# One level of a chunk's triangular block inverse moved from the second to the first stage of a software pipeline

## What is computed

```python
    gdiff = jnp.where(causal, g[..., :, None] - g[..., None, :], 0.0)
    decay = jnp.where(causal, jnp.exp(gdiff), 0.0)
    k_beta = k * beta[..., None]
    lower = jnp.where(strict, jnp.einsum('bhncd,bhnsd->bhncs', k_beta, k) * decay, 0.0)
    rhs = jnp.concatenate([v * beta[..., None], k_beta * jnp.exp(g)[..., None]], axis=-1)
    sol = lax.linalg.triangular_solve(lower, rhs, left_side=True, lower=True, unit_diagonal=True)
    u, w = sol[..., :dv], sol[..., dv:]
    intra = jnp.where(causal, jnp.einsum('bhncd,bhnsd->bhncs', q, k) * decay, 0.0)
    def step(state, inp):
        u_i, w_i, q_i, k_i, a_i, cd_i = inp
        v_new = u_i - jnp.einsum('bhcd,bhde->bhce', w_i, state)
        o_i = jnp.einsum('bhcd,bhde->bhce', q_i, state) + jnp.einsum('bhcs,bhse->bhce', a_i, v_new)
        state = state * cd_i[..., None, None] + jnp.einsum('bhcd,bhce->bhde', k_i, v_new)
        return state, o_i
```

## Time and profile before

| what | value |
|---|---|
| median of 3 runs | 1527.27 us (1525.84 to 1528.35) |
| span of the profiled execution, first to last instruction | 1523.0 us |
| TensorE busy | 1427.9 us, 94% |
| VectorE busy | 674.3 us, 44% |
| GpSimd busy | 624.9 us, 41% |
| ScalarE busy | 452.2 us, 30% |
| mean granted TensorE clock | 0.965 of full speed |

### The profile page before, as it was taken

One profiled execution on the slowest core, in us unless ns is written; L12 is line 12 of the kernel. 1 busy time (PEld: TensorE's weight loads), 2 busy tenths in 40 slices (PEclk: granted clock), 3 DMA queues, 4 the chain that ended last, 5 costly groups with the idle time before them and its releaser, 6 DMA issues.

```text
span 1523.0 us, 18439 instructions
## 1 busy us (share of the span) xinstructions
PE 1427.9 (94%) x7019; PEld 1191.1 (78%) x7019; DVE 674.3 (44%) x857; ACT 452.2 (30%) x516; POOL 624.9 (41%) x359
## 2 busy tenths in 40 slices
PE   3899999999979999889979999999999999999996
PEld 3477878878768999876858888888888888888884
DVE  3825152342656666435553343424243342343426
ACT  3326345351722222133323131221212122131223
POOL 4357667586724111114335252433425234252430
PEclk8799999999989999979989999999999999999998
DMA  8043424233110001101102111111201112111102
GB/s 334 16 125 95 106 56 130 69 89 90 55 56 1 1 0 55 56 28 40 58 0 71 41 56 41 41 41 51 73 28 55 41 41 69 41 55 41 41 28 111
DMA packets 122348, 92.36 MB, mean 61 GB/s; under 512 B 3903, under 2 KB 110668, under 8 KB 122316
## 3 DMA queue, kind: packets, MB, share of 16 engines
q1 hardware_dynamic: 122316, 91.94, 20.0%
HBM read 87.73 MB, written 4.19 MB: 60 GB/s over the span
## 4 chain that ended last, share of the span: by engine, by line
PE 81%; DVE 8%; ACT 5%; issue 3%; DMA 2%; POOL 1%; SPq 0%; POOLq 0%; DVEq 0%; ACTq 0%
PE ps L1497 22%; PE ps L1499 22%; PE ps L1498 22%; PE ps L1623 5%; PE ps L1642 3%; PE ps L1639 2%; DVE sq_lo L1190 1%; DMA ada_first<-in_ada_w_dram 1%; PE ps L1529 1%; DVE ada_first L1103 1%; DVE sq L1187 1%; DVE x L1477 1%; DMA x_hi<-in_x_dram 1%; ACT sq L832 1%; ACT L832 1%
## 5 line engine op out<-in xcount | busy, mean ns | idle before, releaser
L1497 PE MATMUL ps<-h,w_split 128*128 128x512 f32 x448 | 177.4, 396 | 0.0
L1498 PE MATMUL ps<-h,w_split 128*128 128x512 f32 x448 | 176.8, 395 | 0.0
L1499 PE MATMUL ps<-h,w_split 128*128 128x512 f32 x448 | 176.7, 394 | 0.0
L1168 DVE SCALAR_TENSOR_TENSOR cu<-ps,col_c,cu 128x1023 f32<-128x1023 f32 (+1 forms) x44 | 56.4, 1282 | 217.2 <-ACT cu L827 214.3
L1455 DVE TENSOR_TENSOR x<-x,ps 128x512 f32<-128x512 f32 x160 | 107.2, 685 | 76.9 <-PE ps L1499 76.9
L1497 PE MATMUL ps<-wd_split,act_split 128*128 128x512 f32 x352 | 137.9, 392 | 3.2 <-POOL act_split L750 3.2
L1497 PE MATMUL ps<-h,wg_split 128*128 128x512 f32 x352 | 137.8, 391 | 2.2 <-POOL h L623 2.2
L1499 PE MATMUL ps<-wd_split,act_split 128*128 128x512 f32 x352 | 137.7, 391 | 0.0
L1498 PE MATMUL ps<-wd_split,act_split 128*128 128x512 f32 x352 | 137.5, 391 | 0.0
L1499 PE MATMUL ps<-h,wg_split 128*128 128x512 f32 x352 | 137.4, 390 | 0.0
L1498 PE MATMUL ps<-h,wg_split 128*128 128x512 f32 x352 | 137.4, 390 | 0.0
(11 more groups left out here) (272 smaller groups left out, 2811.4 us busy)
## 6 DMA issues: line engine op xcount, KB each, us to landing
ada_raw<-in_ada_w_dram SPq DMA_DIRECT2D x32, 512.0 KB, 4.0
w_raw<-in_w_in_dram SPq DMA_DIRECT2D x28, 512.0 KB, 5.2
wg_raw<-in_w_up_dram SPq DMA_DIRECT2D x22, 512.0 KB, 5.0
wu_raw<-in_w_up_dram SPq DMA_DIRECT2D x22, 512.0 KB, 3.8
wd_raw<-in_w_down_dram SPq DMA_DIRECT2D x22, 512.0 KB, 3.3
ada_first<-in_ada_w_dram SPq DMA_DIRECT2D x4, 2048.0 KB, 17.4
x<-in_x_dram SPq DMA_DIRECT2D x4, 1024.0 KB, 5.9
out_dram<-x SPq DMA_DIRECT2D x8, 512.0 KB, 2.6
```

Source lines behind the costliest of these rows:

```text
L1168: dve.scalar_tensor_tensor(out=dst[:, lag:L], in0=src[:, 0:L - lag], scalar=weight, in1=dst[:, lag:L], op0=ALU.mult, op1=ALU.add).then_inc ...
L1497: pe.matmul(dst, a_hi, b_hi, start=(first and n == 0), stop=False)
L1498: pe.matmul(dst, a_hi, b_lo, start=False, stop=False)
L1499: mm = pe.matmul(dst, a_lo, b_hi, start=False, stop=(last and n == len(pairs) - 1))
```

## The change

The list of levels done in stage a grows from level 1 to levels 1 and 2. Stage b keeps levels 3 to 6 in place of 2 to 6.

```diff
-        A_LEVELS = [1]
-        B_LEVELS = list(range(2, LEVELS))
+        A_LEVELS = [1, 2]
+        B_LEVELS = list(range(3, LEVELS))
```

## The result

The changed kernel takes 1548.06 us in the median of 4 runs (1545.28 to 1549.82), the kernel before 1526.55 (4 runs, 1524.55 to 1528.35): 1.0146 times as long, 95% interval 1.0127 to 1.0165. It is slower, as forecast, but by 21.5 us and not by 6.9, and it lies outside the range (1529.5 to 1545.5). The first rival (the clock falls in the loop) is what happened, and at a higher rate than the forecast gave it.

A forecast was written before the change was run, and what follows sets the result against it. The prediction took TensorE's waits and clock to bound the kernel. Loop +8.4, first step +7.4 and end -8.9 summed to +6.9 us, giving 1534.2 us from 1527.3, range 1529.5 to 1545.5.

The forecast's parts named there:

- The first rival: Clock falls in some loop steps because each has two waits of about 1 us: 1542 us, chance 0.25.
- What bounds the kernel: Delta stage: TensorE sets the pace, busy 25.01 of 26.20 us; only its idle time or clock changes a step.
- Part 1, the loop: End of steps 1 to 7: A's second level makes each step 1.20 us longer, +8.4 us in seven.
- T of A's second level: T is a level's second matmul group (`pm`,`um`), P its first (`tm`,`lt`); this T was to start at 517.98.
- the prices of 2.84 and 1.94 us: Read from uncovered step 8: 2.84 us from T to the next level's P, 1.94 us from P to T.
- its ends (0.85 to 1.4): Bounds per loop step: 0.85 us if part of VectorE's update runs ahead, 1.4 if cover is absent or VectorE's delay is felt.
- Part 2, the first step: Step 0 gains an uncovered level at half clock; the first P of step 1 comes 7.4 us later.
- The upper end (8.3): First step's upper bound: 8.3 us if the first P of step 1 is still slow, 0.9 more.
- Part 3, the end: Step 8 loses its fifth round, so step 9's third stage starts 6.5 us earlier; -8.9 us up to the first output tile.
- ends of 6.5 and 11.3: Bounds of the saving at the end: 6.5 us with the clock low as before, 11.3 with it high throughout.
- The faster rival: First step +4.9, loop below 0.4 us a step, tail at full clock -11.3: sum -3.6, 1523.7 us; chance 0.04.
- The change does nothing: Level order does not matter since TensorE is full: 1527.3 us; chance 0.15 together with ends paying for the loop.

The follow-up runs named there:

- the turned order: Kernel before the change, its levels unmoved, with A ahead of B in the fourth and fifth round on TensorE and VectorE: 1552.09 us, ratio 1.0192.

## Why the prediction was wrong

**What bounds the kernel** held: TensorE's waits and its clock, nothing else. VectorE, ScalarE and GpSimd opened no wait that wasn't named.

**Part 1, the loop**, is the step that failed. Its chain was right to 0.05 us up to T of A's second level, and the prices of 2.84 and 1.94 us came out as read from step 8. Per step it was 1.39 and not 1.20 where the clock held (27.58 against 26.19), within its ends (0.85 to 1.4). But the sum took this term at the clock of the loop before. The two waits it opened stand in a pair, and the pair took the clock down at the ends of five steps of seven; a step with a fall costs 30.5 - 27.6 = 2.9 us more. Five of these are 14.6. Step 1 ran its first 10 us at the low clock that step 0 left behind, 28.9 us where it was 24.2, 3.3 above the chain's 1.39. 9.7 + 14.6 + 3.3 = 27.6 of the measured 28.1. What failed is thus not the chain of waits but the assumption that the clock of the loop, 1.00, would outlast a second wait beside the first.

**Part 2, the first step**: forecast 450.00 - 442.62 = 7.4, measured 7.4. These rows of after answer to the earlier trace rows and show that the clock stays low while two waits cut TensorE's work:

```profile
436.34 1.97 PE L1639 MATMUL ps<-pm_a,um 128*128 128x64 f32 x8 [0.78 <-DVE pm_a L1246]
...
440.95 2.05 PE L1623 MATMUL ps<-tm,lt 128*128 128x128 f32 x8 [0.94 <-DVE um L1257]
443.78 1.97 PE L1639 MATMUL ps<-pm_a,um 128*128 128x64 f32 x8 [0.78 <-DVE pm_a L1246]
...
447.25 2.02 PE L1676 MATMUL ps<-causal,lt 128*128 128x128 f32 x8
449.06 1.91 PE L1623 MATMUL ps<-tm,lt 128*128 128x128 f32 x8
```

What the step left out is what follows: it priced the low clock only to the first P of step 1, and the clock came back at 459.0. The upper end (8.3) let the low clock last for one group more; it lasted for about 10 us more (449.06 to 459.0). That is the 3.3 us above.

**Part 3, the end**: forecast -8.9 between ends of 6.5 and 11.3, measured -9.2. Rows of after that answer to the earlier trace rows:

```profile
658.72 1.16 PE L1623 MATMUL ps<-tm,lt 128*128 128x128 f32 x8 [0.84 <-DVE um L1257]
...
674.54 1.16 PE L1623 MATMUL ps<-tm,lt 128*128 128x128 f32 x8 [0.84 <-DVE um L1257]
676.48 1.11 PE L1642 MATMUL ps<-um,pm_b 128*128 128x64 f32 x8 [0.78 <-DVE pm_b L1246]
677.42 0.71 PE L1686 MATMUL ps<-ident,vc 128*128 128x128 f32 x2
...
689.99 0.47 PE L1497 MATMUL ps<-wo_split,h 128*128 128x512 f32 x1 [3.37 <-POOL wo_split L623]
```

Step 9 comes 6.5 us earlier (658.72 to 677.42 is 18.70, 624.22 to 649.41 was 25.19), as read. From there to the first tile it takes 12.6 us where it took 15.3: 2.7 saved, since a short fall at 677.5 to 680.9 is all that remained of the low 17 us before. The forecast of 2.4 for this was the middle between two ends and not worked out, so that its nearness is partly luck.

**The rivals.** The clock rival had the right mechanism, and its upper price was near (3.4 us for a fall of twice 3.4 us; 2.9 measured in a step). Two choices were off. I gave it 0.25, on the ground that two of three like waits in step 8 had passed at full clock. I also priced it at three falls in seven steps; at the number seen, its own price would have given 1534.2 + 17 = 1551. The rows allowed more: the first two waits of the earlier trace rows are exactly such a pair, and the clock fell 2.5 us behind it, at the third wait (644.5). The short fall at 139 that gave the lower price stood behind a wait of 2.12 us, longer than any that the change opens. The range, too, left out most of this rival's steps (up to +24 was worked out in the text), though it held a chance of a quarter. Nor was its low side the sum of all the ends: these give 1526.8 to 1538.9, not 1530 to 1538. The rule of the Trainium skill named there, in "TensorE: Matmul & The Clock Gate", section "A second HAM failure mode: psum-queue depth-cycling", describes in kind what came: short idles between groups, and a clock that goes up and down between its two levels. The trace agrees, in five steps of seven (1.00, 0.51, 1.00 in the windows of the changed kernel). I set it below my reading of the loop with one wait, which the earlier trace rows could not decide, as the text itself said.

The faster rival asked that P of A's second level start ahead of 2.84 us; at full clock it started 2.84 to 2.85 us after T in the traces of the changed kernel, with fillers or without. "The change does nothing" is out as well.

## What to carry over

When a change opens a short wait on TensorE, don't only add up the waits: look whether it comes to stand next to another one, since a pair of waits of 1 us around a 1 us group cost more here through the clock (2.9 us in each of the five steps that fell) than through the chain (1.4 in every step). Where such a wait can't be closed, put matmuls in it, useful ones if they leave no hole behind, else idle ones; test this first on the kernel that you already have, for here it gave 12 us without any change of the algorithm. Look at the first and last steps of the pipeline too, where cover is missing: that is where falls were left in the filled kernels. A level, tile or stage moved between pipeline stages needs cover in its new place; the equal count of instructions says nothing on that.

## What the runs showed of the hardware

- The granted clock fell after two waits of 0.84 and 0.78 us with a group of 0.9 us between them, while TensorE was counted busy for 93% of the loop (163.44 of 175.00 us). No single long wait was needed.
- It stayed at 0.50 for about 6.8 us after a pair in the loop, though TensorE was busy for all 7.00 us of the window around it, and from 435.1 to 459.0 at the start of the stage.
- A pair doesn't always do it: two of seven passed in the changed kernel's trace, and two of seven with the turned order in the kernel before. The pair at the end of step 7 in the changed kernel passed although a third wait of 0.84 followed it (658.72). Nor is a pair always needed: a fall followed one wait of 0.85 at 497 with the second wait filled, and one of 0.84 at 636 with both filled. Each time only the usual wait of 0.40 ahead of the joint P's stood before it in that step's end. What decides between them is not shown by these runs.
- Four float32 matmuls of 64 columns take as long as four of 128: 0.94 against 0.95 us at full clock (518.67 - 517.73 and 519.62 - 518.67 in the earlier trace rows), and (447.25 - 443.78) / 2 = 1.74 against 538.25 - 536.44 = 1.81 at half. T isn't cheaper than P per matmul.
- Idle matmuls of ones placed in waits did not delay the group behind them (2.84 and 2.85 us from T to P without and with the filler).
